# Sample attention of a decoder step: scores and values as 32-column tiles with four samples side by side

## The reference: what is computed

```
s_s = einsum(q[b], k_sel[b])        # 16 heads x 256 past keys, selection branch
s_w = einsum(q[b], k_win[b])        # 16 heads x 256 past keys, window branch
p   = masked_softmax(s - slope * distance)
o[b] = gate0 * p_c @ vc[b] + gate1 * p_s @ v_sel[b] + gate2 * p_w @ v_win[b]
```

## Time and profile before

| what | value |
|---|---|
| runs of the kernel (3) | 1375.67, 1376.95, 1380.04 us; median 1376.95 us |
| profiled execution, own time | 1382.43 us |
| its span, first to last instruction | 1380.8 us |
| mean granted TensorE clock | 0.977 of full speed |
| PE busy | 1306.5 us (95%) |
| DVE busy | 1055.2 us (76%) |
| ACT busy | 920.7 us (67%) |
| mean DMA rate | 284 GB/s |

### The profile page before, as it was taken

One profiled execution on the slowest core, in us unless ns is written; L12 is line 12 of the kernel. 1 busy time (PEld: TensorE's weight loads), 2 busy tenths in 40 slices (PEclk: granted clock), 3 DMA queues, 4 the chain that ended last, 5 costly groups with the idle time before them and its releaser, 6 DMA issues.

```text
span 1380.8 us, 21526 instructions
## 1 busy us (share of the span) xinstructions
PE 1306.5 (95%) x7292; PEld 1109.1 (80%) x7292; DVE 1055.2 (76%) x1539; ACT 920.7 (67%) x1353; POOL 73.0 (5%) x74
## 2 busy tenths in 40 slices
PE   4998999996998999899999999999999999999996
PEld 4988999996966677678888888888788888887874
DVE  5776555458423487689899899898998998998985
ACT  5535444445372287478798788887987987887863
POOL 0010000004200000020000000000000000002500
PEclk9999999998998999999999999999999999999998
DMA  8399544455565001679999899899998998998930
GB/s 328 130 379 402 187 180 181 177 197 175 187 218 187 1 1 48 288 299 421 363 392 409 318 419 396 332 417 370 352 413 326 404 406 323 416 394 320 408 146 32
DMA packets 59280, 391.50 MB, mean 284 GB/s; under 512 B 6639, under 2 KB 12915, under 8 KB 20627
## 3 DMA queue, kind: packets, MB, share of 16 engines
q1 hardware_dynamic: 50578, 354.29, 65.2%
q0 software_dynamic: 8640, 36.40, 7.2%
HBM read 367.41 MB, written 27.45 MB: 286 GB/s over the span
## 4 chain that ended last, share of the span: by engine, by line
PE 84%; DVE 9%; ACT 3%; issue 3%; DMA 0%; ACTq 0%; DVEq 0%
PE bank L1710 16%; PE bank L1712 16%; PE bank L1711 16%; PE bank L1381 8%; PE bank L1382 8%; PE bank L1383 8%; DVE w_lo L1263 2%; PE bank L1695 1%; PE bank L1509 1%; PE bank L1594 1%; PE bank L1567 1%; ACT w_hi L756 1%; DVE rstd L856 1%; ACT arena L662 1%; PE bank L1555 1%
## 5 line engine op out<-in xcount | busy, mean ns | idle before, releaser
L1263 DVE TENSOR_TENSOR w_lo<-raw,w_hi 128x1024 fp32r<-128x1024 f32 x528 | 623.2, 1218 | 37.1 <-ACT w_hi L756 19.7
L756 ACT CAST w_hi<-raw 128x1024 fp32r<-128x1024 f32 x528 | 543.0, 1055 | 95.3 <-PE bank L1712 94.4
L1710 PE MATMUL bank<-w_hi,xg_hi 128*128 128x512 f32 x704 | 275.2, 391 | 1.4 <-DVE w_lo L1263 1.4
L1712 PE MATMUL bank<-w_hi,xg_lo 128*128 128x512 f32 x704 | 274.3, 390 | 0.0
L1711 PE MATMUL bank<-w_lo,xg_hi 128*128 128x512 f32 x704 | 273.9, 389 | 0.0
L897 DVE TENSOR_TENSOR d_lo<-ring,d_hi 128x1024 fp32r<-128x1024 f32 x120 | 146.6, 1223 | 102.6 <-ACT d_hi L576 102.4
L1381 PE MATMUL bank<-hA_hi,d_hi 128*128 128x264 f32 x640 | 187.9, 294 | 21.1 <-DVE hA_lo L887 15.2
L1382 PE MATMUL bank<-hA_lo,d_hi 128*128 128x264 f32 x640 | 185.3, 289 | 0.0
L1383 PE MATMUL bank<-hA_hi,d_lo 128*128 128x264 f32 x640 | 184.9, 289 | 0.0
L576 ACT CAST d_hi<-ring 128x1024 fp32r<-128x1024 f32 x120 | 125.4, 1046 | 58.5 <-PE bank L1383 55.0
L1710 PEld LDWEIGHTS bank<-w_hi,xg_hi 128*128 128x128 f32 x704 | 132.3, 188 | 29.3 <-DVE w_lo L1263 2.1
(11 more groups left out here) (320 smaller groups left out, 1611.0 us busy)
## 6 DMA issues: line engine op xcount, KB each, us to landing
raw<-in_moe SPq DMA_DIRECT2D x264, 1024.0 KB, 6.8
ring<-in_wd SPq DMA_DIRECT2D x30, 2048.0 KB, 8.5
out_rows<-zeros POOLq DMA_DIRECT2D x1, 6656.0 KB, 62.1
slot_rows<-zeros POOLq DMA_DIRECT2D x1, 6144.0 KB, 44.9
out_rows<-yrow POOLq DMA_DIRECT2D x8, 512.0 KB, 7.8
xs<-slot_rows POOLq DMA_DIRECT2D x7, 512.0 KB, 3.6
arena<-in_cmp_pages POOLq DMA_DIRECT2D x16, 128.0 KB, 2.5
X2v<-in_cmp_pages POOLq DMA_DIRECT2D x16, 128.0 KB, 2.8
```

The source lines that it names most:

```text
L756: nc.scalar.copy(w_hi[:, i % NSPLIT, :], raw[:, u % NRAW, ITEM * (i % 2):ITEM * (i % 2) + ITEM])\
L1263: V.tensor_tensor(w_lo[:, i % NSPLIT, :], raw[:, (i // 2) % NRAW, ITEM * (i % 2):ITEM * (i % 2) + ITEM], w_hi[:, i % NSPLIT, :].bitcast(F3 ...
L1710: T.matmul(out, lhs_hi, hi, start=first, stop=False)
L1712: return T.matmul(out, lhs_lo, hi, start=False, stop=last)
```

## The change

Scores: the 16 calls of a branch no longer write all 128 partitions. Partitions 32 g to 32 g + 31 hold samples 2g and 2g+1. Each call now takes the 32 weight columns of that pair, writes these 32 partitions, and streams the keys of one of the two samples; the four groups g are issued in turn. Four calls accumulate in each group (2 samples, 2 halves of the contraction). The number of calls stays 16 a branch.

Values: each call takes 32 weight columns (a pair of samples) and writes 32 partitions of B[0]; columns 0 to 255 are made with the values of the even sample of each pair, columns 256 to 511 with those of the odd sample. Half of what is written is a product of one sample's weights with the other's values and is not used. The number of calls stays 32.

Results: one bank, copied by one ACT instruction of 128x512. DVE's two copies are gone. The 8 identity products of each half c become 2, each with 128 rows and 64 streamed columns, picked by `by_half` from the identity.

```
-        orow = arena[0:NH, qz_at:qz_at + NS * 2 * P]
+        orow = arena[:, qz_at:qz_at + 4 * P]
...
-            for j in (0, 2):
-                act.wait_ge(orow_done, j + 1)
-                nc.scalar.copy(orow[:, 512 * j:512 * j + 512], B[j][0:NH, :]).then_inc(orow_ready, 1)
+            act.wait_ge(orow_done, 1)
+            nc.scalar.copy(orow[:, :], B[0][:, :]).then_inc(orow_ready, 1)
...
-            for j in (1, 3):
-                dve.wait_ge(orow_done, j + 1)
-                V.tensor_copy(orow[:, 512 * j:512 * j + 512], B[j][0:NH, :]).then_inc(orow_ready, 1)
...
-                for j in range(16):
-                    i = T.matmul(B[n][:, 0:PAST], Qz[:, j % 2, j // 2, :], keys[:, j // 2, j % 2, :], start=(j == 0), stop=(j == 15))
+                for j in range(4):
+                    for g in range(4):
+                        b, rows_ = 2 * g + j // 2, slice(32 * g, 32 * g + 32)
+                        i = T.matmul(B[n][rows_, 0:PAST], Qz[:, j % 2, b, rows_], keys[:, b, j % 2, :], start=(j == 0), stop=(j == 3))
...
-            for b in range(NS):
-                out = B[b // 2][0:NH, 256 * (b % 2):256 * (b % 2) + 256]
+            for half in range(2):
                 for j in range(4):
-                    i = T.matmul(out, PTs[:, j, b * NH:(b + 1) * NH], vals[j // 2][:, b, j % 2, :], start=(j == 0), stop=(j == 3))
-                if b % 2:
-                    i.then_inc(orow_done, 1)
+                    for g in range(4):
+                        rows_ = slice(32 * g, 32 * g + 32)
+                        i = T.matmul(B[0][rows_, 256 * half:256 * half + 256], PTs[:, j, rows_], vals[j // 2][:, 2 * g + half, j % 2, :],
+                                     start=(j == 0), stop=(j == 3))
+            i.then_inc(orow_done, 1)
+
+            def by_half(ap, half):
+                return ap.rearrange("p (g i h) -> p i g h", i=2, h=NH)[:, half]
...
-                    pe.wait_ge(orow_ready, 4)
-                for b in range(NS):
-                    T.matmul(rows_[:, b * NH:(b + 1) * NH], orow[:, 256 * b + c * P:256 * b + c * P + P], ident[0:NH, 0:NH],
+                    pe.wait_ge(orow_ready, 1)
+                for half in range(2):
+                    T.matmul(by_half(rows_, half), orow[:, 256 * half + c * P:256 * half + c * P + P], by_half(ident, half),
                              start=False, stop=False, skip_group_check=True)
```

## The result

The changed kernel took 1357.82 us (median of four runs, 1354.31 to 1359.06), the kernel before 1377.87 us in the same comparison. The ratio is 0.985, interval 0.983 to 0.987: 1.5% faster. A second comparison with five runs gave 0.984 (0.982 to 0.986).

What follows compares the result with a forecast made beforehand. PE was taken to bound the kernel, with 35.7 us of touched products on the chain. Terms -3.44 - 3.44 - 6.68 - 4.0 + 0 + 0.5 = -17.1 us, from median 1376.95 to 1359.9 us; range 1351 to 1372.

Steps and rivals of the forecast that it cites:

- four at once: Rival for scores and values: all four column groups run together, -23.9 us in all, 1353.1 us; chance 0.20.
- The score calls, two at once: First-branch scores: 17 steps of 0.2155, 3.66 us against 7.10, 3.44 us less; likeliest case, chance 0.53.
- the next call's first product can't start before that second one: Scores: products start in order of issue, so only neighbouring calls' halves overlap, one step for each call.
- The second scores: Second-branch scores: likewise 3.44 us less, keeping the 1.68 us of lower clock in the 8.78 us.
- The values: Value products: 33 steps, 7.11 us, plus 1.49 us of clock kept, against 15.28; 6.68 us less.
- the kept term: Value products: 1.49 us of lower clock, as PE comes from idleness, assumed to stay after the change.
- the clock rival: Scores, values and the rest: PE granted the lower level all through, only -5.3 us, 1371.7 us; chance 0.07.
- The copy: Results copy: one ACT copy of 128x512, 0.58 us, covered by 0.83 us of lines 1600 and 1601; cost 0.
- The identity stage: Identity products and what follows up to head 2's scores: 4.0 us less, products at 0.125 us each.
- Changing to tiles and back: Six switches between whole array and tiles, at most 0.164 us each, 1.0 in all; 0.5 us taken.
- Nothing late next: No new wait before compressed values or values; projection tile might land 4 us later, still before its use.
- Loads in the open: Rival for the 128 tile products: weight loads not hidden, +8.9 us, 1385.9 us, or 1407; chance 0.07.

Runs made afterwards that it cites:

- two calls in a row: Changed kernel with values issued as two calls of one column group, then two of the next, and scores as two groups in turn; single run 1360.13 us.
- scores alone: Kernel before with only the loop of the scores replaced by 32-column tiles; 1371.46 us, ratio 0.994 to the kernel before.
- the filled one: Kernel before with unused identity products in two PE gaps, five before head 0's prompt scores and six before the values; 1378.37 us, ratio 0.999.
- the other execution: Changed kernel, nothing altered, timed again in later rounds beside kernels with filled gaps; 1356.77 us.
- group by group: Changed kernel with the two inner loops swapped in scores and values, all four calls of a column group before the next group; single run 1365.74 us.
- five orders: Score-call orders at full clock: four groups in turn 1.86 us, two in turn 2.75, three calls in a row (worked out ahead) 3.23, group by group 4.53, whole array 7.10.

## Why the prediction came out as it did

The forecast was 1359.9 us, the range 1351 to 1372; 1357.8 was measured. The sign, the place and the size were right. The mechanism taken as likeliest was not, and that the sum came so near is partly luck: four at once instead of two gave some 7 us more than forecast (1.8 in each branch of scores, 3.5 in the values), and the lower clock in the values, with prompt scores and an identity stage that were longer than forecast, took some 4 back. The range rests on firmer ground, as it took in four at once on purpose.

- *The score calls, two at once.* Wrong. The step that failed is "the next call's first product can't start before that second one", which assumed starts in the order of issue. Across column groups there is no such order. Four at once had been priced at 5.0 to 5.4 us less a branch; the first scores gave 5.24. The Trainium skill's sentence that products start strictly in program order ("TensorE: Matmul & The Clock Gate", Part 3, What overlaps and what doesn't) disagrees with the runs: in the order with two calls in a row, the values took 6.57 us as against 6.56 in the changed kernel, which they couldn't in strict order.
- *The second scores.* 1.68 us of lower clock had been kept; in this profile there were none (6.92 us less). The change did not take them away: with scores alone the same stretch went at 0.52, and the kernel before has it at 8.78 us or, in the filled one's trace, at 7.10. This part of the 6.92 is luck.
- *The values.* 6.68 us less forecast, 8.72 measured. Two terms were off: four at once took 3.45 us more off than two (7.11 against 3.66), and the clock, kept at 1.49 us, cost 6.56 - 3.66 = 2.9. At half speed half of the time is lost, so 2.9 means some 5.8 us at the lower level here, and 1.49 means 3.0 in the kernel before. In the other execution the clock cost 4.99 - 3.66 = 1.3, and the kept term fits; why the lower level lasts longer in one than in the other isn't shown. "Four at once" alone, at -23.9 us, would have been too much; the clock took part of it back, as the clock rival said, but not in the scores.
- *The prompt scores of heads 0 and 1* weren't in the sum: 1.2 us longer, at 0.56, against 0.68 before. Nor were the small products behind the scores, 0.4 us longer.
- *The copy* cost nothing, as forecast: line 716 ran 0.59 us from 439.00, under lines 1602 and 1603.
- *The identity stage.* 4.0 us less forecast, 2.8 measured in this execution and 439.98 to 443.67, 3.4, in the other. Products with 64 columns took 0.59/4 = 0.148 instead of 0.125 each.
- *Changing to tiles and back.* 0.5 us taken of a bound of 1.0. Measured: 0.14 above the 8 steps and 0.20 behind them, for each branch of scores, and 0.21 above the 16 steps of the values, so 0.9 in all, near the upper bound. How much of it is the change of tiles isn't shown: the whole-array scores also stand 0.20 above their 32 steps.
- *Nothing late next.* Held. No new wait stands before the compressed values or the values (PE idles 2.8 us for DVE before the values, as it did before); the window values still landed 8.5 us after their issue at 412.01, so the projection tile beside them cost them nothing, where 4 us had been allowed.
- *Loads in the open.* Did not happen; six loads stood beside four products on the same 128 rows (the window at 412.02), and three beside eight (413.00). The Trainium skill's rule (same page and section) that a load runs beside products only if its row group differs, taken alone, doesn't hold for these column tiles.

## What to carry to other kernels

In this kernel, small-output fp32 products that stream different data took a quarter of their time as 32-column tiles, if calls to different column groups alternate within two calls of each group; by the model, a third call in a row holds up everything behind it. When a stretch on PE is shortened, look at the clock of what remains: what was a small share at the lower level may now be all of it. Where PE waits idle before such a stretch, unused products that end within the wait can pay: 5.0 us here, but nothing that could be measured in the kernel before, whose values are nearly four times as long.

## What was not expected of the hardware

- fp32 products on four column groups of the array run at the full rate of four: 32 in 1.86 us, against 7.10.
- PE issues past a busy column group: the 9th product of the list started with the 5th (group by group, one product every 0.2155 us until 0.89 us, two from then on), and with two calls in a row the 13th with the first. That a group holds the weights of two calls is inferred from five orders' times, one of them worked out in advance; the trace doesn't name the group that a load goes to.
- The same kernel had its values at 6.56 us in one execution and 4.99 in another, and the same score stretch stood at 1.86 or 3.39 by the clock. A single trace tells such a stage no better than 2 to 3 us (39.1 against 36.4).
